# Reordering the start and three later borders of a two-layer diffusion backbone kernel: token loads issued by ScalarE, tables behind the second filter layer, evacuations and coefficient tables in another order

## The reference, cut to what matters

```
for l in range(2):
    m_lat, m_ctx = adaln(c, ada_w[l], ada_b[l]), adaln(c_ctx, ...)   # silu(cond) @ w + b, 9 groups of 1024
    x = half_ffn(x, m[0], m[1], m[2], ...)      # modulate, SwiGLU with D_FF 2816, gate, residual, layernorm
    x = mixer(x)                                # l=0: Hyena (long conv through FFT tables) + RG-LRU; l=1: MLA attention
    x = layernorm(ALPHA * x + m[5] * y)
    x = half_ffn(x, m[6], m[7], m[8], ...)
# Hyena's filters, before any token is needed:
h = sin(freq0 * (feats @ w1 + b1)); h = sin(freq1 * (h @ w2 + b2)); h = (h @ w3) * window
```

## Time and profile before

| | before |
|---|---|
| median of three executions | 2900.94 us |
| the profiled execution's own time | 2900.35 us |
| its span | 2898.6 us |
| mean granted TensorE clock | 0.991 of full |
| TensorE busy | 2827.6 us (98% of the span) |
| VectorE / ScalarE / GpSimd busy | 69% / 36% / 10% |
| read from memory | 259.98 MB |

### The profile page before, as it was taken

One profiled execution on the slowest core, in us unless ns is written; L12 is line 12 of the kernel. 1 busy time (PEld: TensorE's weight loads), 2 busy tenths in 40 slices (PEclk: granted clock), 3 DMA queues, 4 the chain that ended last, 5 costly groups with the idle time before them and its releaser, 6 DMA issues.

```text
span 2898.6 us, 46273 instructions
## 1 busy us (share of the span) xinstructions
PE 2827.6 (98%) x17255; PEld 2458.2 (85%) x17255; DVE 2010.4 (69%) x3261; ACT 1040.3 (36%) x1646; POOL 285.7 (10%) x395
## 2 busy tenths in 40 slices
PE   7999999999999999999999999999999999999998
PEld 3789999988866888999988889999878998878887
DVE  4677677776767577776776877777767886554545
ACT  2423232335641432232324333332266665422223
POOL 1000100011000101000000000000005553000000
PEclk8999999999999999999999999999999999999999
DMA  6643532221222234444421122222310101233331
GB/s 246 208 131 123 173 96 66 72 66 47 62 88 87 74 117 149 141 152 152 138 73 52 59 70 68 65 65 67 95 42 25 27 19 44 74 115 89 100 101 45
DMA packets 300656, 266.89 MB, mean 92 GB/s; under 512 B 30744, under 2 KB 256664, under 8 KB 300409
## 3 DMA queue, kind: packets, MB, share of 16 engines
q1 hardware_dynamic: 277912, 186.08, 21.7%
q0 software_dynamic: 21760, 76.03, 7.5%
q10 hardware_dynamic: 864, 3.15, 0.3%
HBM read 259.98 MB, written 5.24 MB: 92 GB/s over the span
## 4 chain that ended last, share of the span: by engine, by line
PE 88%; DVE 5%; DMA 3%; ACT 2%; issue 1%; POOL 0%; ACTq 0%; DVEq 0%; POOLq 0%; SPq 0%
PE PSALL L2977 15%; PE PSALL L2978 14%; PE PSALL L2979 14%; PE PSALL L3294 8%; PE PSALL L3295 8%; PE PSALL L3296 8%; PE PSALL L3049 2%; PE PSALL L2882 2%; PE PSALL L3050 2%; PE PSALL L3051 2%; PE PSALL L3722 2%; PE PSALL L3707 1%; DMA ADA<-in_ada_w_dram 1%; PE PSALL L3002 1%; PE PSALL L3587 1%
## 5 line engine op out<-in xcount | busy, mean ns | idle before, releaser
L2071 DVE SCALAR_TENSOR_TENSOR X<-PSALL,GATE,X 128x512 f32<-128x512 f32 x480 | 279.9, 612 | 101.8 <-PE PSALL L2979 101.2
L3294 PE MATMUL PSALL<-HHI,WSH 128*128 128x384 f32 x816 | 273.5, 335 | 5.8 <-DVE HLO L2269 5.8
L3295 PE MATMUL PSALL<-HLO,WSH 128*128 128x384 f32 x816 | 273.5, 335 | 0.0
L3296 PE MATMUL PSALL<-HHI,WSL 128*128 128x384 f32 x816 | 272.7, 334 | 0.0
L2977 PE MATMUL PSALL<-GHIA,WHIW 128*128 128x512 f32 (+1 forms) x618 | 217.9, 353 | 12.8 <-DVE X L2071 9.7
L2978 PE MATMUL PSALL<-GLOA,WHIW 128*128 128x512 f32 (+1 forms) x618 | 213.7, 346 | 0.0
L2979 PE MATMUL PSALL<-GHIA,WLOW 128*128 128x512 f32 (+1 forms) x618 | 213.3, 345 | 0.0
L2977 PE MATMUL PSALL<-GHIB,WHIW 128*128 128x512 f32 (+1 forms) x618 | 213.0, 345 | 0.0
L2978 PE MATMUL PSALL<-GLOB,WHIW 128*128 128x512 f32 (+1 forms) x618 | 213.0, 345 | 0.0
L2979 PE MATMUL PSALL<-GHIB,WLOW 128*128 128x512 f32 (+1 forms) x618 | 212.9, 345 | 0.0
L1182 ACT ACTIVATE WSH<-RAW 128x512 fp32r<-128x512 f32 x204 | 129.1, 633 | 220.7 <-DVE RAW L2148 149.7
(11 more groups left out here) (427 smaller groups left out, 7102.9 us busy)
## 6 DMA issues: line engine op xcount, KB each, us to landing
RAW<-in_ffn_w_in_dram SPq DMA_DIRECT2D x176, 512.0 KB, 4.3
ADA<-in_ada_w_dram POOLq DMA_DIRECT2D x144, 512.0 KB, 5.7
RAW<-in_ffn_w_out_dram SPq DMA_DIRECT2D x88, 512.0 KB, 3.7
RAW<-in_ev_w_in_dram SPq DMA_DIRECT2D x20, 512.0 KB, 4.1
WRAW<-in_mla_w_q_up_dram SPq DMA_DIRECT2D x16, 288.0 KB, 3.0
RAW<-in_ev_w_out_dram SPq DMA_DIRECT2D x8, 512.0 KB, 4.3
RAW<-in_mla_w_in_dram SPq DMA_DIRECT2D x8, 512.0 KB, 4.4
RAW<-in_mla_w_out_dram SPq DMA_DIRECT2D x8, 512.0 KB, 4.7
```

Of the source, the lines that this page charges most:

```text
L2071: dve.scalar_tensor_tensor(X[:, m, lo:lo + n], down_bank(m, s, 2), GATE[:, j, m, s:s + 1], X[:, m, lo:lo + n], ALU.mult, ALU.add).then_inc ...
L3294: te.matmul(out, w_hi, hi[block](k), start=(k == 0), stop=False)
L3295: te.matmul(out, w_hi, low[block](k), start=False, stop=False)
L3296: x = te.matmul(out, w_lo, hi[block](k), start=False, stop=(k == 3))
```

## The change

The instructions are the same except for a few waits. Their order changes, on every engine, in three places.

Start: the six token loads leave SyncE for ScalarE, ahead of all its other work. SyncE waits for the second filter layer before the transform tables and the raw weights behind them. GpSimd waits for the four filter inputs before its first ADA load. TensorE takes tiles 0 and 1 before modulation group 0 and tiles 2 to 5 directly behind the second filter layer, and the filter rows and spectra change places with modulation work. ScalarE does the second sine before the last token take and before the modulation row.

Ends of ffn0, ffn1, ffn2: two evacuations come before `gate_second`, two more before `rebuild_mix(1)`, and `tables` comes behind all sixteen.

Border after attention: the squares' sums come later in TensorE's steps, one weight split moves into the squares on ScalarE, the last chunks and splits move on VectorE, and the second half of `residual` moves behind the first splits of ffn3.

```diff
-               "ln4": (0, 1, (4, 5, 6, 7, 8, 9, 9, 10), 12)}
+               "ln4": (0, 1, (7, 8, 8, 9, 9, 10, 10, 10), 12)}
 # sync
-        for t in range(TB):
-            src = ...
-            sp.dma_start(XIN[:, t, :], src).then_inc(xin_in[XIN_PART[t]], 16)
         sp.dma_start(WINT[:, :, :], A["win"]).then_inc(xin_in[2], 16)
+        sp.wait_ge(f_pe, 2)
         for b in range(LB // 2):
             sp.dma_start(FWDL[:, b, :, :, :], A["flt_l"][b]).then_inc(tab_in, 16)
 # gpsimd
+        pool.wait_ge(flt_in, 16 * 4)
         for g in range(ADA_FIRST):
             ada_loads(0, g, g)
 # scalar
+        for t in range(TB):
+            src = ...
+            act.dma_start(XIN[:, t, :], src).then_inc(xin_in[XIN_PART[t]], 16)
...
-        for e in range(2):
+        for e in range(4):
             x_take(e)
         filter_sine(0)
-        for e in range(2, 8):
+        for e in range(4, 2 * TB - 1):
             x_take(e)
+        filter_sine(1)
+        x_take(2 * TB - 1)
         ada_take(0)
-        filter_sine(1)
-        for e in range(8, 2 * TB):
-            x_take(e)
...
             for m in range(KC):
                 square(0, m)
-            if name == "ln4":
-                next_unit(nxt, "B", (0,))
+                if name == "ln4" and m == 4:
+                    next_unit(nxt, "B", (0,))
...
         even_take(0, 1)
+        ada_take(1)
         act.wait_ge(tr_taken, plan["ada_first"].tr)
         next_unit("ffn0", "A")
         spectra_out(0)
         even_take(1, 0)
-        ada_take(1)
-        even_take(1, 1)
-        spectra_out(1)
         act.wait_ge(coef_ok, COEF_FIRST - 1)
         for m in range(KC):
             h_make(0, "h0", 0, m)
-            if m == 2:
+            if m == 1:
+                even_take(1, 1)
+            if m == 3:
+                spectra_out(1)
+            if m == 4:
                 even_take(2, 0)
-            if m == 5:
-                even_take(2, 1)
-                spectra_out(2)
+        even_take(2, 1)
+        spectra_out(2)
 # vector
         coefs(0, 0)
         co_wait()
-        combine(1, 1)
...
-        for m in range(3):
+        for m in range(2):
+            low("h0", 0, m)
+        combine(1, 1)
+        for m in range(2, 5):
             low("h0", 0, m)
         combine(2, 0)
-        for m in range(3, 6):
+        for m in range(5, KC):
             low("h0", 0, m)
         combine(2, 1)
-        for m in range(6, KC):
-            low("h0", 0, m)
... (last iteration of a wide FFN)
             rebuild_parts(0)
-            if tables is not None:
-                tables()
             up_first("A", last)
             gated_first("A", last)
-            rebuild_mix(1)
+            for e in range(2):
+                accumulate(last - 1, e)
             gate_second("A", last)
             gated_second("A", last)
-            for e in range(4):
+            for e in range(2, 4):
+                accumulate(last - 1, e)
+            rebuild_mix(1)
+            for e in range(4, 6):
                 accumulate(last - 1, e)
             rebuild_parts(1)
-            for e in range(4, 6):
+            for e in range(6, 8):
                 accumulate(last - 1, e)
             split_lo("B", 0, q, last)
-            for e in range(6, 10):
+            for e in range(8, 12):
                 accumulate(last - 1, e)
             split_lo("B", 1, q + 1, last)
-            for e in range(10, 16):
+            for e in range(12, 16):
                 accumulate(last - 1, e)
+            if tables is not None:
+                tables()
... (border after attention)
-            chunk(6, 1)
             next_unit("ffn3", "B", (0,))
-            context("ln4", {0: lambda: chunk(7, 1)}, 3, lambda: next_unit("ffn3", "B", (1,)))
+            context("ln4", {0: lambda: chunk(7, 1)}, 3, lambda: chunk(6, 1), lambda: next_unit("ffn3", "B", (1,)))
...
-        residual("ln4", 1, 5)
-        ffn("ffn3", 1, 5, 0, 0, "final", None)
+        residual("ln4", 1, 5, (0,))
+        ffn("ffn3", 1, 5, 0, 0, "final", None, first=lambda: residual("ln4", 1, 5, (1,)))
 # tensor
         vectors()
+        for t in range(2):
+            x_turn(t)
         te.wait_ge(cond_ok, 2)
         ada_products(0, first)
-        x_turn(0)
         filter_layer(1)
-        for t in range(1, 4):
+        for t in range(2, TB):
             x_turn(t)
         ada_products(0, second)
-        x_turn(4)
...
         filter_rows(0)
-        x_turn(5)
-        filter_rows(1)
         te.wait_ge(tr_taken, plan["ada_first"].tr)
         ada_columns(0, 2)
+        filter_rows(1)
+        filter_rows(2)
         ada_products(1, first)
-        for t in range(2, TB):
+        for t in range(3, TB):
             filter_rows(t)
...
-        spectra(1, lambda: ada_products(1, second))
-        ada_columns(1, 2)
+        ada_products(1, second)
+        spectra(1, lambda: ada_columns(1, 2))
```

More of the change, by code:

```diff
@@ L638, in _ @@
             sp.dma_start(dst[:, :], src).then_inc(xin_in[0], 16)
-        for t in range(TB):
-            src = A["x"][0, t * P:(t + 1) * P, :] if t < LB else A["ctx"][0, (t - LB) * P:(t - LB + 1) * P, :]
-            sp.dma_start(XIN[:, t, :], src).then_inc(xin_in[XIN_PART[t]], 16)
         sp.dma_start(WINT[:, :, :], A["win"]).then_inc(xin_in[2], 16)
+        sp.wait_ge(f_pe, 2)
         for b in range(LB // 2):
@@ L1004, in _ @@
     def _(act):
+        for t in range(TB):
+            src = A["x"][0, t * P:(t + 1) * P, :] if t < LB else A["ctx"][0, (t - LB) * P:(t - LB + 1) * P, :]
+            act.dma_start(XIN[:, t, :], src).then_inc(xin_in[XIN_PART[t]], 16)
         act.wait_ge(tr_taken, VT)
@@ L1837, in low, with residual @@
                               HHI[:, m, lo:lo + n].bitcast(F32), ALU.subtract).then_inc(h_lo, 1)
-        def residual(name, S, j):
-            for a in range(parts_of(name)):
+        def residual(name, S, j, halves=None):
+            for a in range(parts_of(name)) if halves is None else halves:
                 lo, n, _ = part(name, a)
@@ L1866, in norm, with context @@
             dve.tensor_tensor(X[:, m, lo:lo + n], X[:, m, lo:lo + n], wide_bank(name, a), ALU.mult).then_inc(ln_n, 1)
-        def context(name, evict, first, behind=None):
+        def context(name, evict, first, behind=None, beside=None):
             inverse(name, 2, 0)
@@ L1874, in context @@
                 norm(name, 2, 0, m)
+            if beside:
+                beside()
             for m in range(KC):
@@ L1907, in _, with ffn @@
         next_unit("ffn0", "B")
-        def ffn(name, S, j, ada, t0, then, nxt, tables=None):
+        def ffn(name, S, j, ada, t0, then, nxt, tables=None, first=None):
             p = plan[name]
@@ L1945, in accumulate @@
                                          X[:, m, lo:lo + n], ALU.mult, ALU.add).then_inc(evac, 1)
-            dve.wait_ge(ln_x, p.h)
             def body(i, last=False, ada=False):
@@ L1988, in ffn @@
                 split_lo(slot, half, p.q + q, 0)
+            if first:
+                first()
+            dve.wait_ge(ln_x, p.h)
             if ada:
```

## The result

Five executions of the changed kernel gave 2877.92 to 2890.28 us, the median is 2882.04 for 2900.94 before. The ratio is 0.9937 with a 95% interval of 0.9923 to 0.9951: 18.9 us less. The forecast was 2877.0 in a range of 2865 to 2890. The profiled execution took 2881.8 us (span 2879.9) for 2900.35, so its own difference is 18.6 us.

A forecast was written before the change was run, and what follows sets the result against it. TensorE, busy 2827.6 of 2898.6 us, was taken as the bound, so only its idle time and half-clock stretches pay. Terms 3.7 + 4.2 + 5.3 + 7.4 + 3.0 = 23.6 us off 2900.35 gave 2877, range 2865 to 2890.

The forecast's parts named there:

- the likeliest case: Whole kernel: the main forecast of 2877 us, all terms gaining, start gains 6 to 19; chance 0.66.
- Vectors at 7.5: Start: vectors, sharing engines with 3 MB of tokens, land at 7.5 us; bounds 5.76, or later by 2.6.
- First half of group 0 at 19.3: Start: 7.05 MB must land before modulation group 0's first half is used, so 19.3 us, before 14.7.
- four tiles in 7: Start: four token tiles of at most 1.97 us, 22.0 to 29; filter row 0 then at 31.0, -3.7.
- Row 0 to the spectra: Filter rows: 20.0 us instead of 24.2, allowing one half-clock stretch of about 7 us; -4.2.
- Spectra to the ADA products: Spectra to the latent part of h: both low-part gaps and the half-clock stretch behind them go; -5.3.
- What is late next is h for the latents: After the spectra: the next late item is h for the latents, 1.4 us a chunk against TensorE's 1.4.
- Ends of the FFNs: Ends of ffn0, ffn1, ffn2: waits before e = 4 go, new gaps of 1.7 us each; 2.7, 5.0, -0.3, together -7.4.
- rival (b): Gaps change place: start gains zero, each new 1.3 us FFN-end gap brings a half-clock stretch; 2896, chance 0.10.
- After attention: Border after attention: root wait -0.73, squares' sums -1.40, fewer interruptions 0.3, half the residual -0.6; -3.0.
- Rival (a): Start: group 0's second half is late too, TensorE idles, half clock returns; 13.4 in all, 2887, chance 0.19.
- Rival (c): Second filter layer to latent part of h: stays at half clock, so slower by 17 us, 2917; chance 0.05.

The follow-up runs named there:

- tok_late: Changed kernel, but ScalarE waits for the four filter inputs before issuing the token loads; 2887.89 us, ratio 0.9955.
- vec_first: Changed kernel with the load of the vectors issued by ScalarE ahead of its token loads instead of by SyncE; 2888.35 us, ratio 0.9942.
- s_only: The start's part of the change alone, on the kernel before; 2895.99 us, ratio 0.998.
- three: Changed kernel, reordered: FFN-end evacuations further forward, second half of residual behind the A block's splits, group 2's second ADA half behind the latent columns; 2878.36 us, ratio 0.9913.
- after_again: The changed kernel once more, unaltered, for a second trace; 2884.78 us, ratio 0.9939.
- f_only: The part at the ends of the wide FFNs alone, on the kernel before; 2897.12 us, ratio 0.9977.
- l_only: The part at the border after attention alone, on the kernel before; 2898.3 us, ratio 0.9984.
- no_hold: Changed kernel without SyncE's wait for the second filter layer ahead of the transform tables; 2889.69 us, ratio 0.9958.

## Why the prediction was right, and where it was off

The median came 5.0 us above the forecast and inside the range; the likeliest case was the one that happened, and its signs (row 0, spectra, the 1.24 us waits, none ahead of e = 4, shorter stretches at 0.50, the wait for X in ffn3 still there) are in the trace. By its steps:

- **Vectors at 7.5.** They landed at 10.4, beyond my bound of two tiles' time (5.76 + 2.6). `tok_late` shows the cause (tokens in the other queue), and `vec_first` that having them earlier brings nothing.
- **First half of group 0 at 19.3.** Its first block came then, its fourth at 23.4: GpSimd's issue waited for the vectors (issued at 10.56, not 7.5), and the four loads landed 1.2 us apart. Of the 4.1 us the next step gave 3 back: **four tiles in 7** took 3.97. The 1.97 us of the earlier trace rows was that of a tile at the low rate; at full rate it is 0.99. Row 0 came at 32.67 instead of 31.0: the term is -2.0 for -3.7.
- **Row 0 to the spectra**: 18.7 us for 20.0, so -5.5 for -4.2. The half level held 3.4 us and the last 1.4 of it, less than the 7 that I allowed. Here this execution was lucky: in `s_only` and `three` the same stretch of the kernel takes 20.7 and 20.6.
- **Spectra to the ADA products**: 30.1 us for 28.5, so -3.8 for -5.3. The gaps ahead of the low parts are gone, as said, but `spectra(0)` ran at the half level again (6.33 us where my sum has 3.7), behind the same 2.47 us wait that I had left standing. I had costed the wait and not the clock behind it.
- **"What is late next is h for the latents"**: the wrong one. Late next was the load for group 2's second half. Closing the gaps brought its products closer to the first half's, 7.8 us instead of 12.3, and the last of four 512 KB loads issued from 74.66 on does not land in that. The wait is 1.4 to 4.4 us in every trace with the new start, and moving the products removed it.
- **Not in the sum**: between 98 and 208 us the trace loses 3.4 us to a raw block of ffn0 that lands late (VectorE waits 3.66 us for it) and the half level behind. In `after_again` only 0.73 us of wait is left there. Its size is a matter of the execution, but with 2.99 at 1099 there it isn't one of this trace alone: 1 to 4 us of this kind stand in both, and waits of 1.7 us and more at 195 us in no trace with the old start.
- **Ends of the FFNs**: 2.6, 4.8 and -0.5, together 6.9 for 7.4; `f_only` measures 5.4 by its median. The mechanism was right to 0.1 us (1.24 ahead of e = 8). The small waits ahead of e = 10 and 12 did not come above 0.2 us, and in no trace with the new ends did one bring a half-level stretch, so rival (b) did not come.
- **After attention**: 5.5 us in the trace for 3.0. RSC and SQ are as forecast. Half the residual brought next to nothing: the wait of 1.49 us at 2529.99 is gone, and 1.41 stand ahead of the gating instead (my sum had 0.6 left over). Four interruptions for seven saved about 1.3 us, not 0.3: from the root's products to the latents' first matmul there are 32.26 us without the waits for 33.57, with the same 332 matmuls. The rest of the surplus is the wait for X, 2.31 for 2.73, and 1.5 us of the half level behind it, which this execution did not have and `after_again` did; `l_only` measures 4.2. Likewise 2.2 us by 2463, where the kernels are the same, are a wait of 1.49 for 2.01 and the stretch behind it that the trace of before had at 2471.

Together: 2.0 us short at 81.50, 1.5 for the load, 3.8 between 98 and 208 (3.4 of them the raw block), 0.5 at the FFN ends, about 1.9 in small waits near 1100, less 2.5 after attention and 2.2 at 2463: 5.0, for the 4.9 by which the traces' difference (18.7) misses the sum of 23.6. So 9.7 us of losses that I did not forecast stand against 4.7 of gains that I did not forecast either. That the median came within 5 us is in that part luck.

Rival (a), tokens only displace ADA, was half true: the first half of group 0 was 8 us late instead of 4.6. It did not decide, because the 3.3 MB held back on SyncE's queue left room for the second half, and `no_hold` is the case in which they don't: 2889.69, near the 2887 worked out for it. Rival (c) did not come.

## What to carry to other kernels

When loads compete in a start, look at which bytes are held back: a wait in front of bytes that are wanted late was worth 5 us to the first filter row here (3.2 by the bytes, the rest by TensorE's rate behind the waits), and one in front of bytes that are wanted early nothing. What it is worth to issue the tokens from ScalarE was not tested alone, by a run that leaves them on SyncE's queue; the one cost that shows is that the vectors land 5 us later. After closing a gap, look at every load that was hidden by it: its time from the issue to the use has shrunk by the gap. Cost a gap like those of 2.3 to 2.5 us here with a clock stretch behind it that may or may not come, and look at two traces of the same kernel before explaining 3 us.

## What the runs showed that I had not expected

- The same wait is followed by a stretch at the half level in one execution and not in another: 2.31 us at 2532.21, matmul behind it 0.50; 2.35 us at 2534.39, matmul 0.79.
- In the start the granted clock does not tell the rate. `vec_first`, busy time by stretch:

```profile
16.00:25.00 9.00, 6.55 (x41) 2.57 (x42) 2.61 (x5) 1.92 (x3) 1.64 (x4) 1.00 1.01 387
25.00:33.00 8.00, 8.00 (x40) 5.85 (x42) 5.29 (x7) 3.78 (x7) 0.47 (x1) 1.00 0.91 318
```

The record says 1.00, but eight ADA products take 1.08 us there and 0.64 in the changed kernel, and the second layer 2.82 for 1.50. In every kernel here the first layer takes 2.79 us; when the engine comes to the full rate differs: by 19.7 us in the changed kernel, at about 31 in `vec_first`, which had idled more. In two stretches of equal length, both at 1.00, go 12 matmuls and then 20:

```profile
29.00:31.00 2.00, 2.00 (x12) 2.00 (x11) 1.93 (x3) 1.24 (x3) 0.00 (x0) 1.00 0.90 313
31.00:33.00 2.00, 2.00 (x20) 1.70 (x22) 1.91 (x3) 1.99 (x4) 0.00 (x0) 1.00 0.84 288
```

Durations of equal matmuls show the rate there, the granted clock doesn't. It differs between executions of one start as well: the second layer takes 1.50 us in the kernel before and 2.82 in `f_only` and `l_only`, whose start is the same.
- A 192 KB load of vectors landed by 5.1 us with no token or ADA load issued yet (`tok_late`) and at 10.4 beside 3 MB of tokens in another engine's queue, with the transfer engines full: twice the time, beside sixteen times its bytes.
